# A two-layer encoder trunk on one core: the norm's factor moves behind the projections, and the work around the router and the layer end is reordered

## The reference

```python
def rmsnorm(x, gain):
    return x * rsqrt(mean(x * x, axis=-1) + EPS) * gain

h = rmsnorm(x, norm_mix[layer])
x = x + (even_mixer(h, ...) if layer == 0 else odd_mixer(h, ...))
h = rmsnorm(x, norm_ffn[layer])
x = x + hierarchical_moe(h, ...)   # top group of 4, top 2 of its 8 experts
...
for e in range(32):
    hid = silu(h @ w_gate[e]) * (h @ w_up[e])          # 1024 -> 512
    y = y + gates[..., e:e + 1] * (hid @ w_down[e])    # 512 -> 1024
```

## Time and profile before

| | us |
|---|---|
| median of 3 runs | 1271.23 (1270.97 to 1271.80) |
| the profiled execution | 1272.89 |
| its span, first to last instruction | 1271.1 |
| PE busy | 1034.8 (81%) |
| DVE busy | 281.7 (22%) |
| ACT busy | 130.0 (10%) |
| DMA, mean over the span | 350 GB/s |

### The profile page before, as it was taken

The page is one execution under the profiler, slowest core; times in us unless marked ns, Lnnn a source line. Parts: engine busy times, 40 slices in busy tenths (PEclk is TensorE's granted clock), DMA queues, the critical chain, the costliest instruction groups (busy, mean ns, idle before and its releaser), DMA issues.

```text
span 1271.1 us, 12286 instructions
## 1 busy us (share of the span) xinstructions
PE 1034.8 (81%) x5118; PEld 457.8 (36%) x5118; DVE 281.7 (22%) x610; ACT 130.0 (10%) x281; POOL 27.4 (2%) x35
## 2 busy tenths in 40 slices
PE   6989899767777768887899899996777687589877
PEld 5665562322321313342266444523223132133422
DVE  1154343211111111120142333631111111011112
ACT  1023310000000000000141011100000000000001
POOL 1320000100000000000000000000000000000000
PEclk9999999987888888988999899998888898799889
DMA  9962557999999999999983216599999999999995
GB/s 334 288 214 90 210 230 308 408 427 428 427 428 428 428 428 428 426 424 428 392 318 146 80 68 257 205 399 427 427 427 428 428 428 427 428 426 427 425 424 211
DMA packets 52222, 444.37 MB, mean 350 GB/s; under 512 B 5021, under 2 KB 7133, under 8 KB 28353
## 3 DMA queue, kind: packets, MB, share of 16 engines
q1 hardware_dynamic: 49328, 438.32, 83.5%
q0 software_dynamic: 2544, 4.70, 1.5%
q10 hardware_dynamic: 288, 0.53, 0.1%
HBM read 442.47 MB, written 2.11 MB: 350 GB/s over the span
## 4 chain that ended last, share of the span: by engine, by line
DMA 49%; PE 41%; SPq 4%; DVE 4%; issue 1%; ACT 1%; DVEq 0%
DMA sb_weights<-moe_w_down 41%; PE psum L1321 39%; DMA sb_weights<-moe_w_up 7%; SPq L473 3%; SPq L478 1%; DMA sb_x<-x 1%; PE psum L1432 0%; PE psum L1340 0%; ACT sb_hn L587 0%; DVE sb_weights L818 0%; DVE sb_small L820 0%; DVE sb_weights L784 0%; DVE sb_x L1226 0%; DVE sb_hT L768 0%; PE psum L1331 0%
## 5 line engine op out<-in xcount | busy, mean ns | idle before, releaser
L1321 PE MATMUL psum<-sb_weights,sb_hT 128*32 128x512 f32 (+2 forms) x2368 | 490.7, 645 | 110.1 <-DMA sb_weights<-moe_w_gate 91.8
L1321 PE MATMUL psum<-sb_weights 128*32 128x512 f32 (+9 forms) x1514 | 319.2, 598 | 67.5 <-DMA sb_weights<-moe_w_down 55.5
L1321 PEld LDWEIGHTS psum<-sb_weights,sb_hT 128*32 128x32 f32 (+2 forms) x2368 | 151.5, 130 | 428.0 <-issue 354.5
L1321 PEld LDWEIGHTS psum<-sb_weights 128*32 128x32 f32 (+6 forms) x1514 | 110.2, 142 | 263.8 <-issue 209.3
L1226 DVE TENSOR_TENSOR sb_x<-sb_x,psum 128x512 f32<-128x512 f32 x88 | 60.2, 686 | 276.3 <-PE psum L1321 276.3
L1321 PE MATMUL psum<-sb_hT,sb_weights 128*128 128x256 f32 (+1 forms) x400 | 91.3, 388 | 0.8 <-DVE sb_hT L768 0.8
L1321 PEld LDWEIGHTS psum<-sb_hT,sb_weights 128*128 128x128 f32 (+1 forms) x400 | 76.0, 192 | 16.2 <-DVE sb_hT L768 2.8
L1321 PE MATMUL psum<-sb_weights,sb_hn 128*128 128x192 f32 (+1 forms) x384 | 66.5, 335 | 12.2 <-issue 12.2
L1321 PEld LDWEIGHTS psum<-sb_weights,sb_hn 128*128 128x128 f32 x384 | 64.5, 203 | 14.8 <-issue 14.3
L1218 DVE COPY sb_weights<-psum 96x512 f32<-96x512 f32 (+1 forms) x22 | 15.1, 687 | 245.5 <-PE psum L1321 245.5
L1213 DVE TENSOR_TENSOR sb_weights<-sb_weights,psum 96x512 f32<-96x512 f32 (+1 forms) x22 | 15.0, 684 | 167.5 <-PE psum L1321 167.5
(11 more groups left out here) (186 smaller groups left out, 360.0 us busy)
## 6 DMA issues: line engine op xcount, KB each, us to landing
sb_weights<-moe_w_gate SPq DMA_DIRECT2D x64, 2048.0 KB, 24.8
sb_weights<-moe_w_up SPq DMA_DIRECT2D x64, 2048.0 KB, 27.1
sb_weights<-moe_w_down SPq DMA_DIRECT2D x58, 2048.0 KB, 27.2
sb_weights<-moe_w_down SPq DMA_DIRECT2D x12, 1024.0 KB, 18.9
sb_weights<-od_w_in SPq DMA_DIRECT2D x6, 2048.0 KB, 19.8
sb_weights<-ev_w_in SPq DMA_DIRECT2D x5, 2048.0 KB, 27.2
sb_weights<-ev_w_out SPq DMA_DIRECT2D x2, 2048.0 KB, 35.5
sb_weights<-od_w_out SPq DMA_DIRECT2D x2, 2048.0 KB, 7.9
```

Of the source, the lines that this page charges most:

```text
L1321: return nc.tensor.matmul(o, l, r, start=start, stop=stop, skip_group_check=True)
```

## The change

1. Mixer norms: PE transposes the raw `x`, DVE multiplies only the gain in; the projection starts before the factor is known. The factor is spread over partitions by two small matmuls (`spread_inverse`), and DVE multiplies it in when it evicts each projection. With that, block j holds 128 neighbouring columns, and the input projections are read as "(j p)" instead of "(p j)". ACT squares half rows.
2. Last round: the transpositions for the next mixer stand between the last down matmuls and around the last scatter, for half rows as they are ready; DVE adds the first half before it copies the second half of the outputs; the final norm and its stores go by half rows; `keep_warm(4)` is gone.
3. `project_out`: the third `turn_x` and the logits of tile 0 stand inside the last output group; five small rank matmuls become four, of which DVE waits for the first two.
4. `gather_round`: the first gather covers only the first round (96 columns); the second round's follows the transposition of the first round's hidden values. The turning of the gates moves behind the first down matmuls.
5. The gate matrices of the second round are loaded in two row halves; the first half waits only for the first four of eight steps of the first gate matmuls (`half_used`).

```diff
-        w_in0 = A["ev_w_in"][0].rearrange("(p j) n -> p j n", j=KT)
+        w_in0 = A["ev_w_in"][0].rearrange("(j p) n -> p j n", j=KT)
@@ second_round, SP
-                for kind in KINDS:
+                for half, (done_sem, count, full) in enumerate(((half_used, layer + 1, held_full),
+                                                                (main.used["gate"], layer * ROUNDS + 1, main.full["gate"]))):
+                    sp.wait_ge(done_sem, count)
+                    rows = slice(half * 4 * HALF, (half + 1) * 4 * HALF)
+                    for k in range(1, LIGHT):
+                        src = A["moe_w_gate"][layer, LIGHT + k].rearrange("(p j) n -> p (j n)", p=P)
+                        sp.dma_start(unit[SLOT["gate"] + k][:, rows], src[:, rows]).then_inc(full, 16)
+                for kind in ("up", "down"):
@@ mixer0, DVE
-                        nc.vector.tensor_scalar(qkT[:, b:b + 2, :].rearrange("p b t -> p (b t)"), bank,
-                                                A_DH ** -0.5 if c in (0, 3) else 1.0, None, ALU.mult
+                        nc.vector.scalar_tensor_tensor(
+                            out=qkT[:, b:b + 2, :], in0=bank.rearrange("p (b t) -> p b t", b=2),
+                            scalar=A_DH ** -0.5 if c in (0, 3) else 1.0,
+                            in1=inv_row[0].unsqueeze(1).to_broadcast([P, 2, SEQ]), op0=ALU.mult, op1=ALU.mult
@@ last round, DVE
+                add_round(s, r + 1, (0, 1))
                 second_half(s, r + 1)
-                add_round(s, r + 1)
+                add_round(s, r + 1, (2, 3))
@@ PE
+            def turn_h(layer, halves):
+                for t, r in halves:
+                    ...
+                    for jj in range(4):
+                        ins = nc.tensor.transpose(psum[:, 2 * r + t, jj * P:(jj + 1) * P],
+                                                  x[:, t, (4 * r + jj) * P:(4 * r + jj + 1) * P], ident)
+            def spread_inverse(layer):
+                for t in range(TILES):
+                    i = 2 * TILES * layer + t
+                    pe.wait_ge(inv_done, 2 * layer + t + 1)
+                    ins = mm(psum[:, 6, t * P:(t + 1) * P], rrms[:, i:i + 1].to_broadcast([P, P]), ident, True, True)
@@ project_out
+                        if i == 3 and at == 4:
+                            turn_x(layer, 1, 0)
+                            pe.wait_ge(wr_scaled, 2)
+                            logits(layer, 0, 0)
+                            logits(layer, 0, 1)
@@ expert_round
+                if first:
+                    gather_round(s, gn, n, 1)
                 ...
                     if columns:
+                        if half and k == 0:
+                            turn_h(1, halves_in(2)[0:2])
                         scatter(s, n, h, half)
+                if columns and k == 0:
+                    turn_h(1, halves_in(2)[2:4])
+                if first:
+                    turn_gates(s, gn, rows)
@@ end of a layer
-                keep_warm(4)
```

More of the change, by code:

```diff
@@ L1251, in group @@
                     else:
-                        light_rounds(s, (ranks, g + 1), r, gn, following="light", alone=alone)
+                        light_rounds(s, (ranks, g + 1), r, gn, following="light", alone=alone,
+                                     first=layer if alone else None)
                         gathered(layer, s, gn + 1)
@@ L1686, in expert_round @@
                     scatter(s, n - 1, 1 - h, 1)
-                if turn:
+                if turn and not first:
                     turn_gates(s, gn, rows)
@@ L1748, in _ @@
             for layer in range(2):
[L1749 to L1750 removed]
                 if layer == 0:
+                    turn_h(0, halves_in(0))
                     pe.wait_ge(t5_loaded, 32)
```

313 lines of the change are left out of this document (197 added, 116 removed).

## The result

The changed kernel takes 1257.59 us (median of 4 runs, 1254.24 to 1264.72; forecast 1256.4) against 1271.51 of the kernel before (1270.97 to 1274.84), a ratio of 0.9887 (95% interval 0.9842 to 0.9931). Its profiled execution took 1256.98, with a span of 1255.2 against 1271.1. On another chip the same kernel gave 0.9894 (0.9866 to 0.9921).

A forecast was written before the change was run, and what follows sets the result against it. Experts wait for bytes, each mixer with its router for computation. Terms -3.5 + 0.5 - 3.6 - 4.3 + 0.5 - 3.6 - 0.8 = -14.8 gave a median of 1256.4 us, range 1252 to 1261.5.

The forecast's parts named there:

- The start: Up to layer 0's first projection matmul: it starts at 13.3 instead of 16.81, -3.5 us.
- The four conditions: Layer 0's first projection needs PE's transpositions and relative-position matmul (13.2), the gain (9.8), its evictions (12.6), first weights (13.3).
- `spread_inverse`: Mixer norms: two added float32 matmuls, four instructions, cost +0.5 us per layer, twice.
- The router: From the last output add to DVE's last logits read: 5.4 us instead of 4.4, +1.0.
- the gather: Before the first gate matmuls: 32 instructions of 96 columns take 3.7 us instead of 5.3, -1.6.
- the ranks: In the router: DVE waits for four instructions rather than ten, and keep-warm matmuls end a quarter earlier, -0.3 us.
- The restart: Second round's weight stream in each layer: it stands earlier, at 204.2 instead of 207.8, -3.6 us per layer.
- Between the layers: From layer 0's last down matmuls to layer 1's first projection: it starts at 638.3 instead of 642.58, -4.3 us.
- Layer 1's mixer: From layer 1's first projection to its output matmuls: only the added factor-spreading matmuls count, +0.5 us.
- The clock's fall between the layers: Rival: without `keep_warm(4)` PE's clock falls there, 1.5 us per 3 us stretch; total 1257.9 to 1259.4; chance 0.2.
- The restart was given back: Rival: PE still holds the stream behind the first round, each layer loses 3.6 us again; total 1263.6; chance 0.08.
- The strided read: Rival: projection weights read across 128-row neighbours load slower, 30 us lost, total 1286; chance 0.04.

The follow-up runs named there:

- e0: The changed kernel, unchanged, run again on another chip: 1260.98 us, ratio 0.9894 to the kernel before.
- e9: The kernel before, with only GpSimd's bias addition split into eight pieces: 1270.99 us, ratio 0.998 to the kernel before.
- e5: The changed kernel with the second round's up loads also in two row halves: 1258.87 us, ratio 0.9882 to the kernel before.
- e4: The changed kernel with the first gather covering both rounds again: 1266.27 us, ratio 0.9939 to the kernel before.
- e3: The changed kernel with the second round's gate loads whole again, behind all first gate matmuls: 1265.52 us, ratio 0.9936 to the kernel before.
- e12: The e8 kernel again, unchanged, on the chip of e11: 1251.78 us, ratio 0.9833 to the kernel before.
- e7: The changed kernel with GpSimd's bias addition in layer 0's mixer split into eight pieces: 1256.37 us, ratio 0.9849 to the kernel before.
- e2: The changed kernel with tile 0's logits and third transposition back behind the last output matmuls, last add before its copy: 1259.31 us, ratio 0.9882 to the kernel before.
- e8: The changed kernel with the edits of e2, e5 and e7 together: 1250.35 us, ratio 0.9826 to the kernel before.
- e10: The changed kernel with the transpositions for both layers' projections made to wait for the norm's factor: 1263.6 us, ratio 0.9932 to the kernel before.
- e11: The e8 kernel plus warming matmuls (`keep_warm(2)`) between the layers: 1250.7 us, ratio 0.9823 to the kernel before.

## Why the prediction was right, step by step

**The start** was mis-sized: 4.1 gained, forecast 3.5. The four conditions lie close together, as the forecast said, but another one ends last. The first weights land at about 12.3 (10.6 behind the request of 1.67) instead of 13.3, and the gain evictions end at 12.06; what PE starts on is the end of its own work behind the second half of `x`, which landed at 8.97 instead of 9.4, 3.7 later. In e0 it was the weights (12.84). With the scatter of e9's start (15.54) the gain is 3 to 4. The slow part moved along; the 16 matmuls of 12.71 take 0.34 each.

**`spread_inverse`**: 0.61 us for four instructions, forecast 0.5. Evictions kept 0.69 (0.75 where the factor is a column).

**The router**: last logits read 35.14 us behind the first output matmul instead of 33.99, +1.15 (forecast +1.0); the gather 3.64 instead of 5.29, -1.65 (forecast -1.6); the remaining -0.22 is the ranks' (-0.3). The instructions with 96 columns take 0.114 each, so the lower bound by columns, and the Trainium skill's 81 ns ("TensorE: Matmul & The Clock Gate", section "Back-to-back issue gap"), did not come about here.

**The restart** is the term that was too large: 2.9 and 3.0 a layer instead of 3.6. The 0.9 lost to the queue ahead of the up loads was right to 0.1 (e5), and so was the gather (e4). The size of the halves was not: I had 3.6 less 0.9, that is 2.7, and e3 gives 2.0 and 2.3. PE frees the first half at 190.55, 3.7 behind the first gate matmul and not 3.5; in e3 the whole is freed 7.1 behind it. That leaves 3.4, less the gap's 0.9, 2.5. The transfers' slow start is not the cause: it is the same for whole and half loads, as I had assumed (e3). Another 0.2 comes from the first gate matmul, which is 0.7 earlier and not 0.9. What takes the last 0.2 to 0.5 on the way to the last down matmuls was not separated.

**Between the layers** it gained 4.8 instead of 4.3: the last add ends 7.1 us behind the start of the last down matmuls (forecast 7.4), the projection 2.45 behind that add (forecast 2.7). DVE there:

```profile
628.44 0.69 DVE L1316 TENSOR_TENSOR sb_x<-sb_x,psum 128x512 f32<-128x512 f32 x1 [0.17 <-PE psum L1416]
629.05 2.48 DVE L826 TENSOR_TENSOR sb_hT<-psum,sb_small 128x512 f32<-128x512 f32 x4
```

**Layer 1's mixer** is where the forecast had the wrong sign, +0.5 against -1.1. Of the change only the spread and the factor at the evictions lie there. A fall of the clock does. Two of the profiles of changed kernels have none in this mixer (e0, e3) and take 126.7; after, with one of some 3 us (16 matmuls of 713.83 in 8.14 where e12 has 7.13), takes 128.2, 1.5 more. In the kernel before the granted clock is 0.50 for nearly 7 us, and not for the 3 that the forecast read from the window in the earlier trace rows; the same 16 matmuls take 9.69 there:

```profile
724.42 9.69 PE L1321 MATMUL psum<-sb_weights,sb_hT 128*128 128x512 f32 x16
```

That is 1.55 more than in after. With the 0.5 of the spread it makes -1.05 of the measured -1.13. Why the fall was longer there is open. The text had foreseen such shifts "of either sign", without a price in the sum.

**The sum** is closer than its parts. The two restarts gave 1.3 less than forecast, and the clock in layer 1's mixer gave 1.6 that was in no term; that these nearly cancel is luck. So is the profiled run: had it been one like e0's, whose layer 0 mixer takes 5.5 more for the reason that e7 shows, the spans would lie 11.4 apart and not 15.9. The ratios of the runs, 0.9887 and on another chip 0.9894 against a forecast of 0.9883, are the firmer evidence.

**The rivals.** The clock's fall between the layers did not happen in the trace of the changed kernel, yet it did in five of the other profiles (e2, e5, e7, e8, e12), costing 1.6 to 1.7 there, as priced (1.5). It was no loss of the change, because a fall of this size came somewhere in layer 1's mixer in ten of twelve profiles of changed kernels: the stretch is 128.2 to 128.4 with one, 126.7 in e0 and e3 without. Those two have it in the router behind instead, where it costs 0.8; e5 and e7 have both. The restart was given back by 0.7 a layer, not 3.6. The strided read cost nothing: the first megabyte took 10.6 us instead of 11.6.

## What to carry over

Where a stretch is bound by bytes, price the moment at which its stream may restart: what was gained or lost there came back at the end nearly whole (e3 to e5). Work moved into an engine's waits ahead of the last step of a chain can lengthen the chain: e2 gave back 1.2 us a layer by undoing it. When equal runs of a kernel scatter, compare two of its own profiles by stretch before explaining an edit with either.

## What the hardware showed that was not expected

**GpSimd holds up VectorE.** In all nine profiles with the one long instruction (before, after, e0 to e5 and e10) the VectorE operation on SBUF operands that falls in beside it ends 0.01 to 0.28 us behind GpSimd's end, after 1.7 to 6.75 us instead of 0.16 to 0.48. Meanwhile VectorE operations with an operand from PSUM take their 0.69 as ever, and so do a reduction from SBUF (0.69) and a reciprocal (0.15). The Trainium skill ("SBUF — State Buffer", section "SBUF: two separate sides") says that VectorE and GpSimd share a port pair as "an **exclusive lock**, not a bandwidth split", held for a whole instruction, and names VectorE operations in a two-port mode, or with two SBUF inputs where GpSimd's operation reads SBUF, as the one here does. The trace agrees for the two-input addition of 128x1 (1.71); the blocked operation of 6.71 has one tensor input from SBUF, so it would have to be in such a mode, which no run here shows. Pieces bound the loss by one piece: no operation there took over 1.10.

**The clock after a wait.** In layer 0's mixer the granted clock fell to 0.50 for 3 to 7 us behind PE's wait for that VectorE operation in all eight profiles of changed kernels with the long instruction (waits of PE of 2.23 to 6.19), and 16 matmuls took 4.79 to 6.15 instead of 3.62. In the four with pieces (e7, e8, e11, e12; waits of 0.69 to 2.08) it stayed at 1.00. So most of what the pieces gave beside a mild hold-up was the clock. The kernel before fell with the long instruction (2.30) and with pieces (e9, 2.01), so the wait's length alone doesn't decide it. What does stays open, and with it why e9 gained less.
